# Hybrid decoder layer on one core: last quarter of narrow jobs' activations turned by TensorE, first rows turned half by half, gates and biases split between ScalarE and VectorE

## The reference, cut to what matters

```python
h    = rms_norm(x, norm_mix);  proj = h @ w_in + b_in
y_conv = b_gate * causal_short_conv(c_gate * u, conv_w)
y_attn = sliding_window_attention(rms_norm(q), rms_norm(k), v, sinks, rel_bias)
x    = x + concat(rms_norm(y_conv), rms_norm(y_attn)) @ w_out + b_out
h2   = rms_norm(x, norm_ffn)
logits = h2 @ w_router + b_router;  top 4 of 32 experts, gates = softmax(top_vals)
for each expert e, for its tokens:
    hid   = h2[toks] @ w1[e] + b1[e]                 # 1024 -> 2048, even columns glu, odd lin
    glu, lin = min(hid[::2], 7), clip(hid[1::2], -7, 7)
    act   = glu * sigmoid(1.702 * glu) * (lin + 1)
    x[toks] += gate * (act @ w2[e] + b2[e])          # 1024 -> 1024
```

## Time and profile before

| | |
|---|---|
| median of three runs | 2076.33 us (2073.55 to 2079.98) |
| profiled execution | 2082.2 us, span 2080.4 us |
| PE busy | 1982.3 us, 95% of the span |
| DVE busy | 1418.9 us, 68% |
| ACT busy | 352.5 us, 17% |
| POOL busy | 238.6 us, 11% |
| moved by DMA | 504.21 MB, mean 242 GB/s |
| mean granted TensorE clock | 0.979 of full |

### The profile page before, as it was taken

The page is one execution under the profiler, slowest core; times in us unless marked ns, Lnnn a source line. Parts: engine busy times, 40 slices in busy tenths (PEclk is TensorE's granted clock), DMA queues, the critical chain, the costliest instruction groups (busy, mean ns, idle before and its releaser), DMA issues.

```text
span 2080.4 us, 30074 instructions
## 1 busy us (share of the span) xinstructions
PE 1982.3 (95%) x10692; PEld 1453.0 (70%) x10692; DVE 1418.9 (68%) x4145; ACT 352.5 (17%) x732; POOL 238.6 (11%) x305
## 2 busy tenths in 40 slices
PE   7899999994999999989999999999999999999996
PEld 6577777772999999989999999834444444444442
DVE  3345545544276677777876777778887888788876
ACT  2122222221011222212222222210000000000000
POOL 1212222211000111110011111110000000000000
PEclk9999999996899999999999999999999999999998
DMA  9411001002956777767788888999999999999992
GB/s 299 102 41 40 20 30 40 30 31 94 334 169 232 233 259 247 271 211 263 266 283 282 301 294 294 324 332 327 366 356 355 368 367 359 358 362 368 367 353 67
DMA packets 238481, 504.21 MB, mean 242 GB/s; under 512 B 7525, under 2 KB 20881, under 8 KB 236257
## 3 DMA queue, kind: packets, MB, share of 16 engines
q1 hardware_dynamic: 224736, 454.93, 61.1%
q0 software_dynamic: 11392, 40.18, 7.8%
q10 hardware_dynamic: 2304, 8.39, 1.0%
HBM read 475.48 MB, written 28.00 MB: 242 GB/s over the span
## 4 chain that ended last, share of the span: by engine, by line
issue 41%; PE 28%; POOL 2%; DMA 2%; DVE 2%; POOLq 0%; ACT 0%; DVEq 0%
PE ps_unit L1601 28%; DMA out_dram<-y_rows,idx_cur 1%; POOL out_dram L1257 1%; POOL x_got L1213 1%; DMA x_got<-h_rows,idx_next 0%; DVE act_T L1422 0%; DVE sig L1420 0%; DVE glu L1412 0%; ACT sig L1280 0%; PE ps_list L1570 0%; PE ps_unit L1582 0%; POOL carrier L1209 0%; POOL out_dram L1225 0%; POOLq L990 0%; DVE match L1325 0%
## 5 line engine op out<-in xcount | busy, mean ns | idle before, releaser
L1601 PE MATMUL ps_unit<-xT,w_slot 128*128 128x136 f32 (+6 forms) x3840 | 528.3, 300 | 16.3 <-issue 15.3
L1601 PEld LDWEIGHTS ps_unit<-xT,w_slot 128*128 128x128 f32 x3840 | 523.0, 198 | 17.6 <-issue 17.5
L1625 PE MATMUL ps_unit<-w_slot,xT 128*128 128x512 f32 x1088 | 477.2, 597 | 8.1 <-DVE xT L1138 8.1
L1625 PEld LDWEIGHTS ps_unit<-w_slot,xT 128*128 128x128 f32 x1088 | 204.5, 190 | 266.3 <-issue 266.3
L1138 DVE STREAM_TRANSPOSE xT<-x_got 32x256 f32<-32x256 f32 x668 | 291.1, 436 | 16.9 <-DMA x_got<-h_rows,idx_next 7.7
L1601 PE MATMUL ps_unit<-act_T,w_slot 128*128 128x136 f32 (+6 forms) x1920 | 264.0, 299 | 7.0 <-DVE act_T L1422 6.7
L1138 DVE STREAM_TRANSPOSE act_T<-act_rows 32x64 f32<-32x64 f32 x1088 | 256.8, 236 | 16.3
L1601 PEld LDWEIGHTS ps_unit<-act_T,w_slot 128*128 128x128 f32 x1920 | 259.5, 191 | 10.0 <-DVE act_T L1422 5.6
L1637 PE MATMUL ps_unit<-w_slot,act_T 128*128 128x512 f32 x544 | 236.5, 592 | 1.3 <-DVE act_T L1138 1.3
L1438 DVE STREAM_TRANSPOSE y_rows<-yT 32x256 f32<-32x256 f32 x396 | 172.6, 436 | 38.9 <-ACT yT L1287 33.5
L1637 PEld LDWEIGHTS ps_unit<-w_slot,act_T 128*128 128x128 f32 x544 | 103.3, 190 | 131.7 <-issue 129.4
(11 more groups left out here) (247 smaller groups left out, 1505.9 us busy)
## 6 DMA issues: line engine op xcount, KB each, us to landing
w_slot<-in_w_dram SPq DMA_DIRECT2D x192, 2048.0 KB, 10.4
b_row<-in_b_dram SPq DMA_DIRECT2D x17, 1024.0 KB, 12.1
b_row<-in_b_dram SPq DMA_DIRECT2D x17, 512.0 KB, 13.6
w_in_sb<-in_w_in_dram SPq DMA_DIRECT2D x12, 512.0 KB, 8.5
x_in<-in_x_dram SPq DMA_DIRECT2D x8, 512.0 KB, 3.5
x_res<-in_x_dram SPq DMA_DIRECT2D x8, 512.0 KB, 4.9
out_dram<-x ACTq DMA_DIRECT2D x8, 512.0 KB, 5.1
h_rows<-h ACTq DMA_DIRECT2D x8, 512.0 KB, 3.2
```

The source lines that it names most:

```text
L1601: last = pe.matmul(ps_unit[p % RING][:, u, 0:n], w, moving[:, k, 0:n], start=(k == 0), stop=(k == KD - 1))
L1625: last = pe.matmul(ps_hid[c], xT[:, k, 0:P], w_slot[:, c, k, :], start=(k == 0), stop=(k == KD - 1))
```

## The change

In the mixer, `token`, `limits` and `marks` are made on VectorE ahead of its first block. In the set-up, ScalarE makes the three casts of the gates and VectorE the two subtractions, the second of them after the job's fields are made. ScalarE copies the turned biases out of PSUM. `first_rows` turns the eight blocks of the first gather when it has landed and the other eight when the second has; ScalarE and VectorE share the four copies into `xT`. In a narrow job VectorE turns quarters 0 to 2 only; TensorE turns quarter 3 with two transposes into a new PSUM tile `ps_act`, after k 0 to 5 of the first half, and ScalarE copies it into `act_T`. ScalarE scales `b2_row` by the gate, after that copy. The diff without declarations and arguments:

```diff
+            nc.vector.scalar_tensor_tensor(out=token[:], in0=cst[:, C_TOK:C_TOK + NB], scalar=32.0,
+                                           in1=cst[:, C_TOK + NB:C_TOK + 2 * NB], op0=ALU.mult, op1=ALU.add)
+            nc.vector.tensor_scalar(limits[:, 0, :], ...)
+            nc.vector.tensor_scalar(marks[:], ...)
...
         @block.scalar
         def _(act):
+            nc.scalar.copy(gate_parts[:, :, 0, :], gates[:]).then_inc(parts_cast[0], 1)
             nc.scalar.copy(iota_b[:], cst[:, C_IOTA:C_IOTA + CAP]).then_inc(counters_copied, 1)
+            act.wait_ge(parts_left[0], 1)
+            nc.scalar.copy(gate_parts[:, :, 1, :], other[:]).then_inc(parts_cast[1], 1)
...
+            act.wait_ge(parts_left[1], 1)
+            nc.scalar.copy(gate_parts[:, :, 2, :], gates[:]).then_inc(parts_cast[2], 1)
+            act.wait_ge(biases_turned, 1)
+            nc.scalar.copy(b1_units[:, :, 0, :], turned[:, :, 0, :]).then_inc(biases_read, 1)
+            nc.scalar.activation(b1_units[:, :, 1, :], turned[:, :, 1, :], ACT.Identity,
+                                 bias=cst[:, C_ONES:C_ONES + 1]).then_inc(biases_read, 1)
+            nc.scalar.copy(b2T[:], ps_flat[1][:, 0:KD * NE]...).then_inc(biases_read, 1)
             act.wait_ge(biases_read, 3)
+            for i in (0, 2):
+                wait(act, x_turned[i], 0)
+                nc.scalar.copy(xT[:, 2 * i:2 * i + 2, :], ps_x[i][:]).then_inc(xT_read, 1)
...
             def narrow_job(t, q):
+                wait(act, last_turned, t)
+                nc.scalar.copy(act_T[:, KD - 2:KD, 0:P], ps_act[:, 0:2, :]).then_inc(actT_ready[W1_LOADS - 1].sem, 1)
+                wait(act, b2_loaded, t)
+                wait(act, cur_ready, q)
+                nc.scalar.activation(b2_row[:], b2_row[:], ACT.Copy, scale=gate_cur[:, 0:1]).then_inc(b2_gated.sem, 1)
...
-            then_wait(v.scalar_tensor_tensor(out=token[:], ...))
-            then_wait(v.tensor_copy(gate_parts[:, :, 0, :], gates[:]))
-            then_wait(v.tensor_tensor(other[:], gates[:], gate_parts[:, :, 0, :], ALU.subtract))
-            then_wait(v.tensor_copy(gate_parts[:, :, 1, :], other[:]))
-            then_wait(v.tensor_tensor(gates[:], other[:], gate_parts[:, :, 1, :], ALU.subtract))
-            then_wait(v.tensor_copy(gate_parts[:, :, 2, :], gates[:]))
+            dve.wait_ge(parts_cast[0], 1)
+            v.tensor_tensor(other[:], gates[:], gate_parts[:, :, 0, :], ALU.subtract).then_inc(parts_left[0], 1)
...
             v.tensor_copy(fields[:, 2:3], first[:]).then_inc(fields_cast, 1)
+            dve.wait_ge(parts_cast[1], 1)
+            v.tensor_tensor(gates[:], other[:], gate_parts[:, :, 1, :], ALU.subtract).then_inc(parts_left[1], 1)
+            dve.wait_ge(parts_left[1], 1)
...
-            for i in range(4):
-                read_xT(0, i)
+            wait(dve, x_turned[1], 0)
+            v.tensor_copy(xT[:, 2:4, :], ps_x[1][:])
+            wait(dve, x_turned[3], 0)
+            dve.wait_ge(xT_read, 2)
+            v.tensor_copy(xT[:, 6:8, :], ps_x[3][:]).then_inc(xT_ready.sem, 1)
...
                     finish_rows(t, c)
-                    turn_act(t, c)
+                    if c < W1_LOADS - 1:
+                        turn_act(t, c)
...
-                wait(dve, b2_loaded, t)
-                v.tensor_scalar(b2_row[:], b2_row[:], gate_cur[:, 0:1], None, ALU.mult).then_inc(b2_gated.sem, 1)
                 wait(dve, b2_gated, t)
...
+            def turn_last(t):
+                wait(pe, rows_ready[W1_LOADS - 1], t)
+                first = (W1_LOADS - 1) % 2 * PW
+                for k in range(2):
+                    last = pe.transpose(ps_act[:, k, :], act_rows[:, first + k * P:first + (k + 1) * P], ident)
+                last.then_inc(last_turned.sem, 1)
...
-                for ks in (range(0, 6), range(6, KD)):
-                    for m in range(2):
-                        second_layer(t, q, m, ks)
+                second_layer(t, q, 0, range(0, KD - 2))
+                turn_last(t)
+                second_layer(t, q, 1, range(0, KD - 2))
+                for m in range(2):
+                    second_layer(t, q, m, range(KD - 2, KD))
...
             def first_rows():
                 pe.wait_ge(biases_read, 3)
-                for i in range(4):
-                    turn_x(0, i)
+                for h, gathered in enumerate((gathered_a, gathered_b)):
+                    wait(pe, gathered, 0)
+                    for i in range(4):
+                        turn_x(i, h)
```

More of the change, by code:

```diff
@@ L137, in mixer @@
           rel_bias, out_norm_conv, out_norm_attn, w_out, b_out, norm_ffn, w_router, b_router, const,
-          cst, tri_b, ones_b, picked, gates, before):
+          cst, tri_b, ones_b, picked, gates, before, token, limits, marks):
     ident = cst[:, C_ID:C_ID + P]
@@ L693, in _ @@
             nc.vector.tensor_copy(ones_b[:], cst[:, C_ONES:C_ONES + P])
+            nc.vector.scalar_tensor_tensor(out=token[:], in0=cst[:, C_TOK:C_TOK + NB], scalar=32.0,
+                                           in1=cst[:, C_TOK + NB:C_TOK + 2 * NB], op0=ALU.mult, op1=ALU.add)
+            nc.vector.tensor_scalar(limits[:, 0, :], cst[:, C_IOTA:C_IOTA + len(SIZES) - 1], float(SIZE_STEP), float(SIZES[0]),
+                                    ALU.mult, ALU.add)
+            nc.vector.tensor_scalar(marks[:], cst[:, C_IOTA:C_IOTA + len(SIZES)], float(P),
+                                    float(P * (2 - len(SIZES))), ALU.mult, ALU.add)
             def one_block(t, more, first=False):
@@ L959, in _, with experts @@
             one_block(NB - 1, False)
-def experts(nc, h2_rows, out_rows, w1, b1, w2, b2, cst, tri_b, ones_b, picked, gates, before):
+def experts(nc, h2_rows, out_rows, w1, b1, w2, b2, cst, tri_b, ones_b, picked, gates, before, token, limits, marks):
     ident = cst[:, C_ID:C_ID + P]
@@ L1008, in experts @@
         place_cur = sb("place_cur", [P, NB])
-        token = sb("token", [P, NB])
         match = sb("match", [P, NB, CAP], BF16)
@@ L1035, in experts @@
         junk_e = sb("junk_e", [P, 3, NE])
-        limits = sb("limits", [P, 2, last_size])
         fields = sb("fields", [P, 3], BF16)
-        marks = sb("marks", [P, len(SIZES)])
         reached = sb("reached", [P, len(SIZES)], BF16)
@@ L1049, in experts @@
         ps_list = ps("ps_list", [P, 512])
+        ps_act = ps("ps_act", [P, 4, P])
         ps_x = ps_unit[2:]
@@ L1070, in experts @@
         rstep = Steps(sem("routing_step"), 0)
+        parts_cast = [sem(f"gate_part_cast{i}") for i in range(3)]
+        parts_left = [sem(f"gate_part_left{i}") for i in range(2)]
         units_cleared = sem("units_cleared")
@@ L1348, in _ @@
             assert SIZES[:-1] == tuple(SIZES[0] + SIZE_STEP * i for i in range(last_size))
[L1349 to L1352, removed]
             dve.wait_ge(ranked, 1)
@@ L1402, in _ @@
             dve.wait_ge(counters_copied, 3)
+            dve.wait_ge(parts_cast[2], 1)
             dve.wait_ge(table_ready, TABLES)
             match_tokens(0, bass.ds(first_expert, 1), base_row[:, 0:1])
-            def read_xT(t, i):
-                wait(dve, x_turned[i], t)
-                v.tensor_copy(xT[:, 2 * i:2 * i + 2, :], ps_x[i][:]).then_inc(xT_read if i < 3 else xT_ready.sem, 1)
             def clip(q, p):
@@ L1572, in list_tokens, with turn_x @@
                 last.then_inc(listed.sem, 1)
[L1574 to L1578, removed]
+            def turn_x(i, h):
                 for c in range(2):
-                    for h in range(2):
-                        k = 2 * i + c
-                        last = pe.transpose(ps_x[i][:, c, h * P:(h + 1) * P], x_got[:, h, k * P:(k + 1) * P], ident)
-                last.then_inc(x_turned[i].sem, 1)
+                    k = 2 * i + c
+                    last = pe.transpose(ps_x[i][:, c, h * P:(h + 1) * P], x_got[:, h, k * P:(k + 1) * P], ident)
+                if h == 1:
+                    last.then_inc(x_turned[i].sem, 1)
             def piece(q, p, n):
@@ L1726, in program @@
         before = ctx.enter_context(nc.sbuf_tensor("before", [P, NB + 1, NE], BF16))
+        token = ctx.enter_context(nc.sbuf_tensor("token", [P, NB], F32))
+        limits = ctx.enter_context(nc.sbuf_tensor("limits", [P, 2, len(SIZES) - 1], F32))
+        marks = ctx.enter_context(nc.sbuf_tensor("marks", [P, len(SIZES)], F32))
         mixer(nc, x_rows, out_rows, h2_rows, rel_rows, norm_mix, w_in, b_in, conv_w, q_norm, k_norm, sinks,
               rel_bias, out_norm_conv, out_norm_attn, w_out, b_out, norm_ffn, w_router, b_router, const,
-              cst, tri_b, ones_b, picked, gates, before)
-        experts(nc, h2_rows, out_rows, w1, b1, w2, b2, cst, tri_b, ones_b, picked, gates, before)
+              cst, tri_b, ones_b, picked, gates, before, token, limits, marks)
+        experts(nc, h2_rows, out_rows, w1, b1, w2, b2, cst, tri_b, ones_b, picked, gates, before, token, limits, marks)
```

14 lines of the change are left out of this document (5 added, 9 removed).

## The result

| | before | changed |
|---|---|---|
| median of the first comparison | 2076.33 us (2073.55 to 2084.77, 5 runs) | 2066.66 us (2063.17 to 2068.67, 5 runs) |
| ratio, 95% interval | | 0.9943 [0.9926, 0.9960] |
| median of a second comparison, another chip | 2076.48 us (9 runs) | 2067.40 us (5 runs) |
| ratio, 95% interval | | 0.9952 [0.9938, 0.9967] |
| span of the profiled execution | 2080.4 us | 2064.8 us |

What follows compares the result with a forecast made beforehand. PE's own work was taken to set the pace in the narrow jobs, with DMA keeping up. Terms 3.5 + 4.4 + 3.0 + 1.45 = 12.3 us took the median from 2076.3 to 2064.0 us, range 2057 to 2072.

Steps and rivals of the forecast that it cites:

- Steady jobs: Narrow jobs: 8.6 us of TensorE's waits for xT saved, 5.1 paid for transposes, net 3.5 us (-4.8 to 5.1).
- xT early: Steady narrow jobs: without the last quarter on VectorE, xT is ready 3.9 us before it is wanted.
- First narrow job: First narrow job: wait for xT gone, new wait of 0.7 for the last quarter's rows; gain 4.4 us (2.6 to 4.4).
- The 1.8 us for the clock: After the first narrow job's wait for xT: 1.8 us gained if the clock stays up.
- Set-up: Set-up before the first job: VectorE reads rank 1.7 us earlier, first gather issued 1.5 earlier; bounds 0.8 and 1.9.
- First rows: First job's rows: first half turned while the second gather lands, so PE starts 1.5 us earlier (0.8 to 1.7).
- End: Last job: gating and first half of y_rows done before PE's end; last scatter 1.45 us earlier (1.2 to 1.5).
- Clock pulled down: Rival, narrow jobs: the transposes lower the clock, 1.8 us each time, 30.6 in 17 jobs; time 2094.6; chance 0.05.
- dear transposes: Rival, narrow jobs: transposes not hidden in the pipeline, 0.84 us a job; gain 4.0, time 2072.3; chance 0.06.
- Code waits dealt anew: Rival, where wide size changes: unexplained PE wait grows (2070.4 us, chance 0.10) or long one shrinks (2057.6, chance 0.07).
- The set-up part: Set-up and first rows together, ahead of the first job: 3.0 us earlier (1.6 to 3.6).
- a shift that is there at the first wide job and gone at the first narrow one: Sign against the prediction: time gained before the wide jobs but lost by the narrow ones would make it wrong.

Runs made afterwards that it cites:

- the narrow part alone: Kernel before the change with only quarter 3 turned by TensorE, copied by ScalarE, and bias row gated on ScalarE: 2067.39 us against 2078.63, ratio 0.9949.
- experiment 2: Changed kernel with its narrow jobs put back to how they were, gating on VectorE too: 2077.00 us against 2078.63 before, ratio 0.9992.
- experiment 4: Changed kernel with GpSimd's clearing of x_got moved ahead of its three DMA issues: one run, 2064.74 us.
- experiment 5: The changed kernel once more, unaltered: 2067.40 us, ratio 0.9952 to the kernel before.
- experiment 3: Changed kernel with ten transposes where there are two in every narrow job: one run, 2080.73 us.
- experiment 6: Changed kernel with x_got's clearing moved first and the last quarter split, VectorE turning one block, TensorE the other: 2067.86 us, ratio 0.9956 to before.
- experiment 8: Changed kernel with VectorE turning all four quarters again, ScalarE still gating the bias row: one run, 2070.79 us.

## Why the prediction was right, point by point

- **Direction, size and place: right.** The forecast terms came to 12.3 us, the same stretches of the two profiles to 14.3, the timings to 9.7, 9.1 and, for the narrow part alone, 11.2. That the sum is this close is in part luck: the steady jobs brought 1.5 more than their term and the set-up 0.95 less, and 1.25 in the profiles are a gather that landed sooner.
- **Steady jobs: 0.57 a boundary, right; the price on PE, 0.32, too dear.** It is 0.22, with no change-over, which was the lower bound. The row of the mixer that I took the extra 0.1 from is followed by 256-column matmuls; behind a 512-column record nothing shows. The period fell 0.35: 15 x 0.57 - 16 x 0.22 = 5.0 us, not 3.5. Here TensorE is the bound, and the wait was worth more than twice what replaced it.
- **xT early: right.** 4.2 us to spare where 3.9 were forecast; nothing else became late in the steady jobs.
- **First narrow job: right as built** (46.61 to 43.97, 2.6 us; the new wait for the last quarter's rows is there, 0.5 idle where 0.7 was forecast). The 1.8 us for the clock came in this pair of traces, as 43.76 - 42.06 = 1.7 in the second job, and would not have against experiment 2's. It was a term to be put in by its chance, not in full. (The rest before it is 3.41 us by the earlier trace rows; the prediction's 3.6 counts from the next start that TensorE could have had.)
- **Set-up: wrong in size, 0.55 instead of 1.5 us, under its own low bound of 0.8.** Rank was read 1.77 earlier as forecast (499.37 - 496.85 against 493.98 - 493.23), and the second subtraction came back as forecast; the bias copies gave the 0.2 (from the subtraction of counts and rank to the list it is 7.13 against 7.33). Missing from my sum was GpSimd: I moved VectorE's line against GpSimd's, which stands still, and did not ask what the two then do at the same time. The collision cost 0.96, which closes the sum (1.77 - 0.45 - 0.96 + 0.20 = 0.56); experiment 4 gets 0.65 of it back net.
- **First rows: right, 1.6 for the 1.5.** The half-wise turning did what was said; another 1.25 was the luck of a gather. The clock rose with the earlier start in this pair, as taken: it was at 0.50 for the first 4.6 us of the job, against 4.2 before. That too was luck. In experiment 5, the same kernel, it was up 1.4 us before the job began (last row below), and over the ten traces it rose anywhere from 1.8 us before that moment to 4.6 after it:

```profile
520.87:525.40 4.53, 4.53 (x13) 0.50 1.05 387
525.50:530.00 4.50, 4.50 (x27) 1.00 1.04 383
```
```profile
521.91:526.40 4.49, 4.49 (x26) 4.49 (x27) 0.18 (x1) 2.77 (x3) 0.00 (x0) 1.00 1.05 388
```

- **End: right, 1.44 for 1.45,** 0.8 of it the gating.
- **The rivals.** Clock pulled down and dear transposes: refuted by experiment 3. Code waits dealt anew: the long one is where it was, 9.73 us against the 9.41 of the earlier trace rows; the wide stage moves by 8 us between traces with no tie to the change, but by at most 2 in TensorE's idle time; up to 6.6 are the half clock, which no rival named for this stage. This is noise on the result and not an effect.
- The set-up part, 3.0 us in the sum and 3.4 in this pair of traces, is in the timing 1.6 (-0.2 to 3.5); the interval includes nothing at all. The prediction named a sign against itself: a shift that is there at the first wide job and gone at the first narrow one. Counted from the stage's start, 3.4 us are there at the first and 1.2 at the second. The split of the wide stage says why: its work is the same, 783.4 us, and 1.7 of the 2.2 us went to the clock and 0.5 to idle time, both of which wander as much with the same code (experiment 5). The shift itself passes through; what it is worth in time is under what these timings resolve.

A version better than the changed kernel would carry experiment 4's edit (0.65 us); it is too little for these timings to show, and with experiment 6's split on top it was no faster. Moving the clearing out of VectorE's way altogether, into the mixer, was not tried.

## What to carry to other kernels

When one engine is busy from end to end, look at what another engine does just before it has to deliver: 0.57 us of waiting a job could be bought off with 0.22 us of the busy engine's own time, and the price is the distance from start to start of such an instruction, not its length. When an engine's line is moved in time, lay the other engines' lines beside it again, above all GpSimd's next to VectorE's; a collision costs without any semaphore. And before a gain of a few us is credited to a change, take the stretches of several traces: here two stretches that the change leaves as they were, but for three small instructions, moved by 5 and 8 us. Where such a stretch has rests in it, split off what the granted clock cost before looking for a cause in the code.

## What the runs showed of the hardware that was not expected

- Ten TensorE transposes in a row between matmuls, 1.09 us, in each of 17 jobs: granted clock 1.00 throughout.
- After a rest of 3.4 us the granted clock fell in two of three traces (before and experiment 8, not 2); after one of 2.04 it fell in the one trace that had it. A fall costs 1.7 to 1.8 us there. In the wide stage TensorE has four rests of over 2.5 us, in all ten traces: after the first (2.5 to 2.9 us) the clock fell in five, after the second (2.8 to 3.2) in five, after the third (8.1 to 9.7) and the fourth (2.5 to 3.4) in all ten. In the first two places the length of the rest does not tell which.
- A stream transpose of 32 x 32 takes 0.22 us on VectorE (3.45/16), one of 32 x 64 0.25 (3.98/16): half the columns save 13%.
- A VectorE compare over 12 columns stood 1.4 us for a GpSimd clearing of 128 x 2048, while a single-column instruction beside it, ahead of the compare, ran at its usual 0.16.
